# The second half's rest of every second stripe moves from VectorE to GpSimd, counted by VectorE

## The reference, cut to what matters

```
q = (xt @ w_q).reshape(n, PEER_HEADS, 2, PEER_HALF)
s = einsum('nhpd,hpkd->nhpk', q, subkeys);  s_top, i_top = top_k(s, 16)
best, sel = top_k(all sums of the two lists, 16);  gate = softmax(best)
a = gelu(einsum('ted,td->te', u[ib], xb));  out = einsum('te,ted->td', gb * a, v[ib])
```

## Time and profile before

| | us |
|---|---|
| three timed runs | 4093.75, 4102.52, 4110.12 |
| median | 4102.52 |
| the profiled execution | 4088.34 |
| its span | 4086.7 |

### The profile page before, as it was taken

One profiled execution on the slowest core, in us unless ns is written; L12 is line 12 of the kernel. 1 busy time (PEld: TensorE's weight loads), 2 busy tenths in 40 slices (PEclk: granted clock), 3 DMA queues, 4 the chain that ended last, 5 costly groups with the idle time before them and its releaser, 6 DMA issues. The chain is left out here.

```text
span 4086.7 us, 69881 instructions
## 1 busy us (share of the span) xinstructions
PE 3873.6 (95%) x26178; PEld 3694.0 (90%) x26178; DVE 3053.1 (75%) x4066; ACT 1422.0 (35%) x2046; POOL 1569.2 (38%) x1350
## 2 busy tenths in 40 slices
PE   7999999999999897999899999999787999999997
PEld 7999988999999665989799999999787999999997
DVE  5875167777777333878678999999876888888887
ACT  5785122222223223233333333333223333333332
POOL 0000022323323112234245666677562555555550
PEclk9999999999999898999899999999899999999998
DMA  6988878999999796889677888898797999999996
GB/s 233 346 313 298 292 282 337 344 356 365 362 361 364 271 385 250 308 322 348 252 281 284 316 321 304 308 329 304 296 391 295 357 344 345 344 345 345 343 343 240
DMA packets 336018, 1310.11 MB, mean 321 GB/s; under 512 B 48880, under 2 KB 105360, under 8 KB 266272
## 3 DMA queue, kind: packets, MB, share of 16 engines
q1 hardware_dynamic: 201648, 646.09, 43.2%
q0 software_dynamic: 108848, 629.71, 41.7%
q10 hardware_dynamic: 25344, 31.99, 2.1%
HBM read 1237.86 MB, written 69.77 MB: 320 GB/s over the span
## 5 line engine op out<-in xcount | busy, mean ns | idle before, releaser
L2356 POOL DMA_INDIRECT routes_scratch<-gate_sums,route x384 | 449.3, 1170 | 117.0 <-issue 117.0
L129 PE MATMUL acc<-x_hi,w_hi 128*128 128x448 f32 x1296 | 477.1, 368 | 10.2 <-DVE x_lo L1363 6.7
L129 PE MATMUL acc<-x_lo,w_hi 128*128 128x448 f32 x1296 | 475.1, 367 | 0.0
L129 PE MATMUL acc<-x_hi,w_lo 128*128 128x448 f32 x1296 | 474.8, 366 | 0.0
L113 ACT ACTIVATE w_hi<-w_raw 128x1024 fp32r<-128x1024 f32 x242 | 256.0, 1060 | 621.3 <-DMA w_raw<-in_w_gate 250.0
L118 DVE TENSOR_TENSOR w_lo<-w_raw,w_hi 128x1024 fp32r<-128x1024 f32 x242 | 295.3, 1222 | 204.2 <-ACT w_hi L113 203.1
L2741 POOL TENSOR_TENSOR tile_full<-act_and_gate 128x320 f32<-128x320 f32 x120 | 318.2, 2652 | 267.3 <-DVE tile_lo L2840 166.5
L2191 PE MATMUL acc<-h_hi,w_hi_b 128*128 128x320 f32 (+1 forms) x1152 | 370.3, 321 | 36.8 <-DVE w_lo_b L2181 36.8
L2173 ACT ACTIVATE w_hi_a<-w_raw 128x1024 fp32r<-128x1024 f32 x272 | 281.1, 1057 | 302.4 <-PE acc L2905 258.4
L2191 PE MATMUL acc<-h_hi,w_hi_a 128*128 128x320 f32 (+1 forms) x1152 | 367.7, 319 | 17.7 <-DVE w_lo_a L2181 17.2
L2173 ACT ACTIVATE w_hi_b<-w_raw 128x1024 fp32r<-128x1024 f32 x272 | 279.7, 1055 | 261.3 <-PE acc L2905 217.8
(11 more groups left out here) (506 smaller groups left out, 10378.0 us busy)
## 6 DMA issues: line engine op xcount, KB each, us to landing
w_raw<-in_w_peer_u SPq DMA_DIRECT2D x256, 512.0 KB, 6.7
w_raw<-in_w_peer_v SPq DMA_DIRECT2D x256, 512.0 KB, 6.0
w_first<-in_w_gate SPq DMA_DIRECT2D x96, 512.0 KB, 4.9
w_raw<-in_w_gate SPq DMA_DIRECT2D x96, 512.0 KB, 7.0
w_first<-in_w_z SPq DMA_DIRECT2D x66, 512.0 KB, 5.2
w_raw<-in_w_z SPq DMA_DIRECT2D x66, 512.0 KB, 7.7
k_ring<-in_cache_k SPq DMA_DIRECT2D x64, 512.0 KB, 6.9
v_ring<-in_cache_v POOLq DMA_DIRECT2D x64, 512.0 KB, 8.5
```

What stands on the lines that cost most here:

```text
L129: last = nc.tensor.matmul(dst, l_, r_[:, cc, 0:cn], start=(cc == first and p_ == 0), stop=(cc == last_c and p_ == 2))
L2356: pool.indirect_dma_start(route_dram, bass.IndirectOffsetOnAxis(ap=route[0:ROWS[b], b, n:n + 1], axis=0), gsum[0:ROWS[b], h % SUMS, b - 1, ...
```

## The change

In 64 odd stripes, from 15 to 141 (`POOL_REST`), VectorE subtracts the first half alone. The second half's subtraction is made by GpSimd (`rest_half`), which waits for the same rounding as VectorE did. It stands in GpSimd's queue ahead of row `rows_ahead_of(s)`: in general row taken_by[s - 2] + 4, or ahead of a head's first gather where the stripe is not behind the one in which that head's rows start. There it also stands ahead of the scatters that belong before this row. VectorE waits for GpSimd's count (`s_plo`) behind its steps of that stripe and ahead of the stripe's late rows, waits for its own first count, and then adds one to `q6["lo"]` by itself, so that SP and PE wait for the same counter as before. The loops of SP, ScalarE and PE stay as they are.

```
+        POOL_REST = [s for s in range(GROUP + 1, NS_ - 1, 2)]
+        def rows_ahead_of(s):
+            for q in range(min(NROWS, taken_by[s - 2] + NROW - 1)):
+                kind, n = order[q]
+                if kind == "u" and n % PTOP == 0 and GROUP * (n // PTOP) + 18 >= s:
+                    return q
+            return min(NROWS, taken_by[s - 2] + NROW - 1)
...
+                def rest_half(n, s):
+                    pool.wait_ge(q6["hi"], 2 * s + 2)
+                    hi, lo = slot(2 * (s % 2) + 1)
+                    nc.gpsimd.tensor_tensor(lo, raw[:, (2 * s + 1) % 4, :], hi.bitcast(F32), ALU.subtract).then_inc(s_plo, 1)
...
                 for q in range(NROWS):
+                    while halves < len(POOL_REST) and rows_ahead_of(POOL_REST[halves]) <= q:
+                        rest_half(halves, POOL_REST[halves])
+                        halves += 1
                     while x < scatters_before(q):
...
                 for s in range(NS_):
-                    if s:
+                    if s in POOL_REST:
+                        j = 2 * (s % 2)
+                        dve.wait_ge(q6["hi"], 2 * s + 1)
+                        nc.vector.tensor_tensor(slot(j)[1], raw[:, j, :], slot(j)[0].bitcast(F32), ALU.subtract).then_inc(q6["lo"], 1)
+                    elif s:
                         split_lo(dve, s // 2, s % 2, q6)
...
                     for h, name in plan.get(s, ()):
                         step(h, name)
+                    if s in POOL_REST:
+                        dve.wait_ge(s_plo, POOL_REST.index(s) + 1)
+                        dve.wait_ge(q6["lo"], 2 * s + 1)
+                        dve.sem_inc(q6["lo"], 1)
                     for q in range(early, taken_by[s]):
                         row(q)
```

More of the change, by code:

```diff
@@ L2261, in build @@
         s_gat = [sem(f"row_gathered{k}") for k in range(NROW)]
+        s_plo = sem("second_rest_by_gpsimd")
         s_used, s_sct, s_gel = sem("row_used"), sem("gates_scattered"), sem("gelu_done")
@@ L2374, in _ @@
                     pool.dma_start(x1_dram[COLS[b]:COLS[b] + ROWS[b], :], x1[0:ROWS[b], b, :]).then_inc(s_park, 16)
+                def rest_half(n, s):
+                    pool.wait_ge(q6["hi"], 2 * s + 2)
+                    hi, lo = slot(2 * (s % 2) + 1)
+                    nc.gpsimd.tensor_tensor(lo, raw[:, (2 * s + 1) % 4, :], hi.bitcast(F32), ALU.subtract).then_inc(s_plo, 1)
                 x = 0
+                halves = 0
                 for q in range(NROWS):
+                    while halves < len(POOL_REST) and rows_ahead_of(POOL_REST[halves]) <= q:
+                        rest_half(halves, POOL_REST[halves])
+                        halves += 1
                     while x < scatters_before(q):
@@ L2380, in _ @@
                     gather(q)
+                while halves < len(POOL_REST):
+                    rest_half(halves, POOL_REST[halves])
+                    halves += 1
                 while x < NSCT:
```

## The result

The change makes the kernel slower. Its median is 4195.26 us (4 runs, 4183.59 to 4198.48) against 4099.01 us of the kernel before measured beside it (4 runs, 4093.75 to 4110.12): ratio 1.0231, 95% interval [1.0204, 1.0259]. Forecast were 4206 us. The profiled executions stand 4192.89 to 4088.34 us, +104.6 where the sum said +106.

What follows compares the result with a forecast made beforehand. PE sets the pace in table u, with GpSimd having about 14 us to spare in 106. Terms 70 + 8 + 15 + 12 + 4 - 3 = +106 us gave 4194 to 4208, stated as 4206; range 4135 to 4300.

Steps and rivals of the forecast that it cites:

- GpSimd has 14 us to spare in 106, not 62%: Table u's stage: per head GpSimd works 92.2 us without pause, then idles 13.7 until VectorE has the next list.
- A rest takes 2.4 us: One second-half subtraction (128x1024) on GpSimd, scaled from 128x320: 2.4 us, bounds 2.2 and 3.7.
- Heads 1 to 6, 70 us: Late gathers and second halves in GpSimd's queue: 13 us each in heads 1 to 4, 9 each in 5 and 6.
- Head 0, 8 us: Subtractions ahead of gather 15 delay its row on VectorE, so PE begins stripe 17 8 us late.
- The last head, 15 us: GpSimd is full and bounds there; seven subtractions of 2.4 are 17 us, 15 of them reach the end.
- The clock, 12 us: PE's stalls lower its granted clock; a head's last stall is not absorbed: 8 x 1.5 = 12 us.
- The scatter that waits for those just issued, 1 us: A head's first scatter waits until all before it have landed: 1 us, four heads, 4 us.
- The place of the count costs nothing: VectorE's count behind its steps costs nothing by itself, unless VectorE is over 1.4 us later.
- VectorE's relief, 3 us: 64 subtractions, 78 us, leave VectorE, mostly hidden under PE; lighter odd stripes give back 3 us.
- Locked out: Rival: GpSimd's subtractions take 3.7 us, half lose another 1 to VectorE's lock: +190, some 4290 us; chance 0.20.
- All hidden: Rival: GpSimd's faster gathers and scatters and the ring of five rows absorb the subtractions: 0 to +20, about 4110; chance 0.07.
- faster: Rival: VectorE sets the pace in heads 4 to 7 and its relief goes to PE: -20, about 4082; chance 0.06.

Runs made afterwards that it cites:

- experiment 6: The changed kernel, unaltered, run again on a chip of a later group: 4209.14 us, 0.9739 of the kernel before beside it.
- Experiment 3: Kernel before plus 64 full-size subtractions on GpSimd on data nobody else uses, not waiting for a rounding: 4197.25 us, ratio 0.9738.
- Experiments 2: Kernel before plus 64 full-size GpSimd subtractions on data nobody else uses, at the change's places, waiting for the same roundings: 4193.14 us, ratio 0.9708.
- experiment 1: Against the changed kernel, VectorE makes both subtractions, still counting the second behind its steps; GpSimd makes none: 4322.13 us, 1.0013 of the kernel before.

## Why the kernel before is slower in the later runs

**9. The kernel before with a trace of its own.** Unchanged.

> The kernel before, unchanged, for a trace of its own beside the other kernels of these chips. The trace of before that the prediction rests on has TensorE waiting 0 us for its accumulators without a releaser. Theory S (TensorE is short of instructions where GpSimd's queue issues gathers and scatters without a break): 4300 to 4330 us, with some 150 us of idle time of TensorE that the profile puts down to issue, in the first pass of PE's loops behind a head's start. Rival R (the longer time is a slower clock or later data all over the program): the same time, issue under 40 us, and the difference spread over the stages.

Measured: 4319.78 us. Its table u, the start of one head in it, and the wait table of PE in the stage:

```profile
1967.10:3358.90 1391.80, 1191.13 (x7143) 1134.27 (x7144) 1025.51 (x1633) 391.30 (x484) 651.32 (x558) 0.90 0.72 260
2243.20:2278.80 35.60, 19.54 (x109) 16.70 (x107) 12.19 (x25) 3.53 (x5) 27.35 (x28) 0.76 0.81 270
```
```profile
PE acc L2191 <- issue: 159.7, 176, 3.0
PE acc L2191 <- DVE w_lo_b L2181: 25.8, 8, 10.1
PE acc L2191 <- DVE w_lo_a L2181: 12.9, 4, 5.7
```

228.3 of the 233.7 us that the span is longer are in table u. There PE is idle 146.7 us more (200.7 for 54.0) and busy 81.6 us more at a granted clock of 0.90 for 0.98. The wait table puts 159.7 us to "issue": nothing that the profile shows ended these waits. I read them as a want of instructions; the profile has no row for an instruction's arrival. The second stretch shows where: GpSimd issues 28 gathers and scatters in 35.6 us without a break, behind a pause of 34 us, and PE is busy 19.5 us. The timeline of PE within it:

```profile
2258.35 0.31 PE L2191 MATMUL acc<-h_lo,w_hi_a 128*128 128x320 f32 x1 [1.67 <-issue]
2259.04 0.31 PE L2191 MATMUL acc<-h_hi,w_lo_a 128*128 128x320 f32 x1 [0.39 <-issue]
2260.46 0.40 PE L2191 MATMUL acc<-h_hi,w_hi_a 128*128 128x320 f32 x1 [1.11 <-issue]
2261.18 0.31 PE L2191 MATMUL acc<-h_lo,w_hi_a 128*128 128x320 f32 x1 [0.31 <-issue]
2263.28 0.42 PE L2191 MATMUL acc<-h_hi,w_lo_a 128*128 128x320 f32 x1 [1.80 <-issue]
```

These matmuls belong to one half of a stripe, between which the program waits for no tile. They start 0.7 to 2.1 us apart, for 0.147 elsewhere. In the first trace of before GpSimd issues 64 in a row in 92 us and PE has no such gap. The change's trace of experiment 6 has 20.5 us of it.

The gaps have fixed places. 127.8 of the 159.7 us lie in seven stretches, at stripes 32, 46, 60, 75, 89, 103 and 116 to 117, each of which begins 13 to 20 us behind the first gather of a head. Six of the seven are also the first pass of one of PE's loops over two stripes (these begin at stripes 4, 18, 32, 46, 60, 74, 88, 102 and 112); the seventh is not, and the loops from 4, 18 and 112 have no gap in their first pass. So PE's own new code could play a part, and no run moves it away from GpSimd's row.

**10 and 11. Small instructions in GpSimd's queue.** Experiment 3 with one column, and with 320; the inputs are cut alike.

```diff
-                    nc.gpsimd.tensor_tensor(spare[:], a_, b_, ALU.subtract).then_inc(s_plo, 1)
+                    nc.gpsimd.tensor_tensor(spare[:, 0:1], a_, b_, ALU.subtract).then_inc(s_plo, 1)
```

> The kernel before, with 64 instructions of one column (0.18 us) on GpSimd at the 64 places of the change, nobody waits for them. Their own time is 64 x (0.18 + what the issue costs), under 30 us. Theory S in the form 'a break of the row of DMA issues is enough': TensorE gets its instructions again, issue idle time falls from 150 to 20 us, and the time is 4130 to 4200. Theory S in the form 'it needs GpSimd's queue to be silent for some time': the time stays within 0.5% of before, 4290 to 4330.

> As the run with one column, with 320 columns (0.87 us each, 56 us in all; the change's 1024 columns are 2.4 us each, 154 us). Break is enough: as with one column plus what GpSimd's time costs a head (64 x 0.7 x 0.7 = 30 us): 4160 to 4230. Silence needed: between before and the change, 4230 to 4290.

**12. The change in every fourth stripe.**

```diff
-        POOL_REST = [s for s in range(GROUP + 1, NS_ - 1, 2)]
+        POOL_REST = [s for s in range(GROUP + 1, NS_ - 1, 4)]
```

> The change with every fourth stripe instead of every second, 32 rests. By the forecast's own step (GpSimd's time and its late gathers set the price) it costs half or less of the change's +104 us against a before without issue idle time. Theory S: the issue idle time is 30 to 90 us, since a break comes half as often, and the two nearly cancel: 4190 to 4260. If only the number of rests counts for the issue idle time (nine rests left it at 137 us): 4240 to 4280.

Measured, with the idle time of PE in table u that the wait table puts down to issue (from one trace each) and the mean length of one instruction:

| on GpSimd | median us | ratio to before beside it | PE "issue" us | stage us |
|---|---|---|---|---|
| none (before) | 4319.78 | 0.999 [0.9962, 1.0019] | 159.7 | 1391.8 |
| 32 rests (every fourth) | 4309.63 | 0.9973 [0.9948, 0.9999] | 122.3 | 1375.2 |
| 64 x one column, 0.39 us | 4277.68 | 0.9901 [0.9873, 0.9929] | 126.6 | 1356.2 |
| 64 x 320 columns, 0.96 us | 4265.11 | 0.984 [0.9793, 0.9888] | 98.4 | 1338.0 |
| 64 x 1024 columns, 2.53 us (3) | 4197.25 | 0.9738 [0.9681, 0.9794] | 15.1 | 1262.2 |
| 64 rests (the change, 6) | 4209.14 | 0.9739 [0.9705, 0.9773] | 20.5 | 1292.8 |

With 64 instructions, longer ones between the issues mean less of this idle time of PE, in steps. "A break is enough" is refuted: one column left 126.6 us where 20 were expected. "Silence is needed" in its strict form is wrong too, since one column gains 1%. Thirty-two rests gain nearly nothing, and my 4190 to 4260 was wrong; that their own price and the little that they relieve cancel is my reading of it.

So the experiments show that in these runs PE's idle time for issue goes with GpSimd's row of indirect DMAs at a head's start, and that 64 subtractions in its queue take most of it away. By which way they do so is open: in the same traces PE's waits for data grow (38.7 us without them, 42.5 and 47.4 with 64 small ones, 104.0 in experiment 3), and a PE that stands still for data may be given its instructions meanwhile. No run holds data back without using GpSimd. Why the first measurement has none of it in the same kernel, they don't show. That stays open; so does the path by which the two engines meet. The better kernel thus depends on it: before, 4099 us, where instructions arrive, and the change, 4209 us to 4315, where they don't. No version tried beats the first 4099.

## Why the prediction was right

The result lies 11 us under the forecast. That the number is so close is in part luck: of the path from GpSimd to PE the forecast had the start and the sum, but not the half of a stripe at which PE would stand, and its terms for idle time and for the clock missed in opposite directions. The comparison is the first pair of traces, which have none of PE's want of instructions. By the forecast's steps, with PE's lag read at a head's like stripes:

- **GpSimd has 14 us to spare in 106, not 62%: right of the kernel before, but the spare time was not filled.** Pauses for the list fell from 135.9 to 14.6 us, the sign that was named, and a period took 122.0 us where 119 were foretold. Yet 14.3 us of it are still idle, now ahead of rests that wait for their rounding. Experiments 2 and 3 reach the change's time with GpSimd's subtractions alone, so their time is enough for the cost, if the kernel before would have taken its 4099 us beside them.
- **A rest takes 2.4 us: right.** Median 2.408, from a scaling of 128x320. The worst is 3.07, under the upper bound of 3.7.
- **Heads 1 to 6, 70 us and their share of the clock: right in sum, wrong in the path.** The lag grew by 15.4, 12.7, 14.2, 11.1, 9.8 and 13.6 us, 76.8 in all, clock and scatters' wait included; the terms for these heads (70, some 9 of the clock's 12, and 4) make 83. The forecast had PE wait for second halves, since the rest is late. Those waits are 19.7 us; waits for first halves grew by 36.3 (44.2 for 7.9 in these heads), and the remaining 21 us are PE's slower matmuls. In head 1 stripe 33 cost 6.4 us where 1.5 were foretold, stripe 35 3.8, and stripe 41 5.0 where the whole 13.5 were to appear. I had reckoned the late gather through GpSimd's queue to the next rest. It acts sooner, through VectorE, which waits for the landing and has nothing to make it up with, the path that the forecast itself priced in head 0; what PE loses there it does not lose again at 41. Heads 5 and 6 were to lose 9 each and lost 9.8 and 13.6.
- **Head 0, 8 us: right**, 7.5, and by the path foretold: stripe 17's first half is 5.6 us late, the rest is the clock.
- **The last head, 15 us: somewhat low.** The lag grew from 84.3 to 103.8, 19.5 us. VectorE's waits for table v's rows rose to 43.0 us.
- **The clock, 12 us: too small a term.** In 6 us around the wait in stripe 33 the granted clock is 0.52, and over the stage PE's busy time grew 26.6 us. So the pure stalls were smaller than their terms: 77 us of idle time for the 97 of 70 + 8 + 15 + 4. The two misses cancel, and that is luck.
- **The scatter that waits for those just issued, 1 us: too small.** It was 2.3 to 3.1 us, three times in all (7.7 us), so the term is 8 for 4.
- **The place of the count costs nothing: not contradicted**, experiment 1, with what is said there. **VectorE's relief, 3 us: not measured by itself.** 78 us were taken from it, yet its busy time in the stage fell only 27.6 (1023.73 to 996.09): L2604 takes 1.560 us in the mean instead of 1.22 (22 us), the first rows of table v 120.5 us for 112.9, and the step that writes the routes 13.3 us for 1.7.
- **The rivals.** "Locked out" fell: GpSimd's rest is hardly lengthened. The lock works the other way, on VectorE, up to 4.129 us for an instruction of 1.22. The Trainium skill (SBUF — State Buffer, section Who interferes with whom) has the later of two such instructions fully blocked. This trace agrees in part. Ten of the 64 first halves on VectorE are lengthened, and each ends 1.08 to 1.09 us behind the end of GpSimd's subtraction. Seven of them had started later than it. The other three, the 4.129 among them, had started up to 0.7 us earlier, while GpSimd was issuing a gather, and were held all the same:

```profile
2615.66 0.98 POOL L2384 DMA_INDIRECT ring<-in_peer_u,eidx  x1 [0.30 <-issue]
2615.97 4.13 DVE L2604 TENSOR_TENSOR w_lo_b<-w_raw,w_hi_b 128x1024 fp32r<-128x1024 f32 x1
2616.65 2.35 POOL L2391 TENSOR_TENSOR w_lo_b<-w_raw,w_hi_b 128x1024 fp32r<-128x1024 f32 x1
```

"All hidden" and "faster" have nothing for them in the first traces. The later runs give a ratio of "faster" by a mechanism that was no rival of mine: against their kernel before the forecast's time was right and its direction wrong.

## What to carry to other kernels

An engine with a low busy share may have little to spare in the stage that counts: add issue times to busy times and compare with the period. When a wait shrinks, look whether another has taken its place: here the pause for the list became a wait for the rounding. A wait put down to whoever came last can hide whom the engine needed; read which instruction stood behind it. In an in-order queue of DMA issues, ask first who consumes what stands behind the new instruction; here the late rows hurt before the late result did, and moving the instruction only moved the loss. Before a ratio is trusted, the kernel before should be measured and traced more than once, on more than one chip: here its time moved by 5% between groups of runs and the change's, measured in two groups, by 0.3%.

## What the hardware showed unexpectedly

- PE can stand idle while nothing that the profile shows holds it: 159.7 us in table u of the kernel before in one trace, none in another of the same kernel. The wait table's "issue" on PE is the row to look at.
- GpSimd's one-column subtraction took 0.210 us in the median in this queue and 0.39 in the mean, since a few took up to 1.535; a one-column copy took 0.178 in the median.
- A short VectorE instruction is hit hard by GpSimd's subtraction: the step that writes the routes (128x64, 8 times, here in the kernel after) takes 1.668 us in the mean, 0.217 before. Four of the eight took 3.1 us, the others 0.22. The four began some 0.6 us ahead of GpSimd's subtraction, during a gather's issue, and ended 0.09 us behind it.

```profile
L2517 DVE SCALAR_TENSOR_TENSOR route<-eid_f,token 128x64 int32<-128x64 f32 x8 | 13.3, 1668 | 0.0
```
